# Hybrid encoder trunk on one core: parameter loads on another queue, two-operand work in another instruction, and other engine orders

## The reference

```python
h = rms(x, norm_g)
p = h @ w_in[layer]                       # 1024 x 11808, cut into the parts below
a = deltanet(conv5(p_qkv), gates(p_ab)) * silu(z_a)     # 4 heads, chunks of 64, both directions
b = neighbourhood_attention(q, k, v, rpb) * silu(z_b)   # 8 heads of 64, 16 columns
c = grouped_query_attention(rope(q), rope(k), v) * silu(z_c)
d = mlstm(q, k, v, gates(p_if)) * sigmoid(o) * silu(z_d)
m = sum over n of sigmoid(h @ w_gate[n]) * (branch[n] @ w_branch[n])
x = x + m @ w_out[layer]
```

## Time and profile before

| | |
|---|---|
| median of 3 runs | 962.58 us (962.46 to 967.27) |
| profiled execution | 968.08 us |
| its span | 966.0 us |
| TensorE busy | 903.6 us (94%) |
| VectorE busy | 660.0 us (68%) |
| ScalarE busy | 496.8 us (51%) |
| GpSimd busy | 208.6 us (22%) |
| granted TensorE clock, mean | 0.988 |

### The profile page before, as it was taken

How to read it: one execution, slowest core, us unless ns; L and a number is a source line. 1 busy time by engine, 2 the same in 40 slices (tenths; PEclk the granted TensorE clock), 3 DMA queues, 4 the chain that set the end, 5 groups by cost and what they waited for, 6 DMA issues and landing times.

```text
span 966.0 us, 18557 instructions
## 1 busy us (share of the span) xinstructions
PE 903.6 (94%) x7206; PEld 745.9 (77%) x7206; DVE 660.0 (68%) x1205; ACT 496.8 (51%) x997; POOL 208.6 (22%) x220
## 2 busy tenths in 40 slices
PE   0899989999999999999999999899999999999998
PEld 0798868787778788877879887687777777887786
DVE  0579895656437888568766989655644777875874
ACT  1546753554445466535545666344543555655452
POOL 0201521135240100322120122213334010032310
PEclk9999999999999999999989999899999999999999
DMA  7473544434339535548657346343333693443764
GB/s 214 128 231 114 179 136 130 116 91 127 118 92 215 142 98 174 143 132 213 201 153 227 101 161 208 91 131 89 88 111 110 164 208 99 142 144 100 216 196 109
DMA packets 101964, 141.03 MB, mean 146 GB/s; under 512 B 31102, under 2 KB 45558, under 8 KB 101750
## 3 DMA queue, kind: packets, MB, share of 16 engines
q1 hardware_dynamic: 97995, 138.76, 49.7%
q10 hardware_dynamic: 3883, 1.10, 0.6%
HBM read 136.67 MB, written 7.27 MB: 149 GB/s over the span
## 4 chain that ended last, share of the span: by engine, by line
PE 72%; DVE 15%; ACT 3%; DMA 3%; ACTq 2%; POOL 2%; issue 2%; SPq 1%; POOLq 0%; DVEq 0%
PE pj L764 14%; PE pj L766 13%; PE pj L765 13%; DVE w_low L1563 5%; PE pair L758 4%; PE mb L764 4%; PE mb L766 3%; PE mb L765 3%; DMA ring<-in_w_in 2%; DVE big L1632 2%; PE pair L964 2%; ACTq L719 2%; PE mb L1104 1%; PE pair L959 1%; PE mb L758 1%
## 5 line engine op out<-in xcount | busy, mean ns | idle before, releaser
L1563 DVE TENSOR_TENSOR w_low<-ring,w_high 128x512 fp32r<-128x512 f32 x460 | 324.4, 747 | 85.1 <-ACT w_high L1271 84.0
L1271 ACT ACTIVATE w_high<-ring 128x512 fp32r<-128x512 f32 x460 | 277.2, 629 | 189.0 <-PE pj L766 120.9
L764 PE MATMUL pj<-w_high,h_high 128*128 128x512 f32 x584 | 238.4, 408 | 4.9 <-DVE w_low L1563 4.9
L766 PE MATMUL pj<-w_high,h_low 128*128 128x512 f32 x584 | 228.4, 391 | 0.0
L765 PE MATMUL pj<-w_low,h_high 128*128 128x512 f32 x584 | 228.2, 391 | 0.0
L764 PEld LDWEIGHTS pj<-w_high,h_high 128*128 128x128 f32 x584 | 110.0, 188 | 33.0 <-DVE w_low L1563 7.0
L766 PEld LDWEIGHTS pj<-w_high,h_low 128*128 128x128 f32 x584 | 109.8, 188 | 24.1
L765 PEld LDWEIGHTS pj<-w_low,h_high 128*128 128x128 f32 x584 | 110.3, 189 | 21.0 <-issue 0.5
L1276 ACT ACTIVATE big<-pair 128x512 f32<-128x512 f32 (+2 forms) x136 | 61.1, 481 | 78.7 <-PE pair L948 47.1
L2058 POOL TENSOR_TENSOR big<-big,tab 128x256 f32<-128x256 f32 x40 | 35.4, 894 | 127.8 <-PE pair L948 70.3
L2156 POOL TENSOR_TENSOR zbuf<-zbuf,mid 128x512 f32<-128x512 f32 x20 | 30.5, 1532 | 102.8 <-DVE mid L1977 102.8
(11 more groups left out here) (291 smaller groups left out, 1621.5 us busy)
## 6 DMA issues: line engine op xcount, KB each, us to landing
ring<-in_w_in SPq DMA_DIRECT2D x368, 256.0 KB, 3.4
ring<-in_w_branch SPq DMA_DIRECT2D x64, 256.0 KB, 3.3
ring<-in_w_out SPq DMA_DIRECT2D x32, 256.0 KB, 3.3
big<-skew SPq DMA_DIRECT2D x32, 128.0 KB, 4.9
skew<-lines SPq DMA_DIRECT2D x16, 224.0 KB
out_x<-btm SPq DMA_DIRECT2D x8, 256.0 KB, 3.9
btm<-out_x SPq DMA_DIRECT2D x8, 256.0 KB, 5.6
tab<-in_table SPq DMA_DIRECT2D x1, 1408.0 KB, 12.3
```

The source lines that it names most:

```text
L764: mm(o, r32(a), r32(b), start=start, stop=False, skip_group_check=True)
L766: return mm(o, r32(a_low), r32(b), start=False, stop=stop, skip_group_check=True)
L1271: f(r32(part(u, 0)), ring[:, u % RAW], ACT.Copy).then_inc(w_rounded, 1)
L1563: tt(r32(part(u, 1)), ring[:, u % RAW], part(u, 0), ALU.subtract).then_inc(w_split, 1)
```

## The change

Three things are changed.

1. The loads at the start. ScalarE's queue keeps only the identity and `norm_g`. The taps go to SyncE behind unit 5. The table, the narrow columns and the ten parameters go to SyncE as well, each behind one weight unit: the table behind unit 8, the columns behind unit 9, the parameters behind units 10 to 19.
2. Every `tensor_tensor` on VectorE becomes a `scalar_tensor_tensor` that first multiplies the first operand by 1.0. This includes the 464 subtractions of L1563.
3. The orders of the four engines are other ones, in both layers (both run one and the same order).

```diff
-        def load_rows(queue, layer):
+        def load_gain(queue, layer):
             queue.dma_start(g_row, norm_g[layer][None, :].to_broadcast([P, D])).then_inc(g_row_in, 16)
+        def load_taps(queue, layer):
             queue.dma_start(rawp[0:CONV * CB, :], conv_a[layer].rearrange("j (b c) -> (j b) c", c=P)).then_inc(colp_in, 16)
...
                 for unit in range(2, RAW):
                     load_unit(sp, unit)
-                sp.dma_start(tab[:, P:n_const], table[:, P:n_const]).then_inc(table_in, 16)
+                load_taps(sp, 0)
...
                 act.dma_start(tab[:, 0:P], table[:, 0:P]).then_inc(ident_in, 16)
-                load_rows(act, 0)
-                load_cols(act, 0)
+                load_gain(act, 0)
...
                         load_unit(sp, unit)
+                        first = unit - RAW - 2
+                        if layer == 0 and 0 <= first < PARAMS + 2:
+                            if first == 0:
+                                sp.dma_start(tab[:, P:n_const], table[:, P:n_const]).then_inc(table_in, 16)
+                            elif first == 1:
+                                load_cols(sp, 0)
+                            else:
+                                load_param(sp, 0, first - 2)
...
-                    if layer == 0:
-                        for n in range(PARAMS):
-                            load_param(act, 0, n)
...
-                    tt, ts, stt, reduce = nc.vector.tensor_tensor, nc.vector.tensor_scalar, nc.vector.scalar_tensor_tensor, nc.vector.tensor_reduce
+                    ts, stt, reduce = nc.vector.tensor_scalar, nc.vector.scalar_tensor_tensor, nc.vector.tensor_reduce
+
+                    def join(o, one, other, op):
+                        return stt(o, one, 1.0, other, ALU.mult, op)
...
-                            tt(r32(part(u, 1)), ring[:, u % RAW], part(u, 0), ALU.subtract).then_inc(w_split, 1)
+                            join(r32(part(u, 1)), ring[:, u % RAW], part(u, 0), ALU.subtract).then_inc(w_split, 1)
```

Of the orders, the beginning and two places of TensorE's, and ScalarE's and VectorE's beginning:

```diff
-        turn_h.0.0 turn_h.0.1 turn_h.1.0 taps turn_h.1.1 za:0:0+4@0 za:0:4+2@0 za:0:6+2@0 za:0:0+2@1 za:0:2+4@1 za:0:6+2@1 conv:0:0+4 conv:1:0+4
-        conv:2:0+4 conv:3:0+4 gatecols c:0:0+2 gatecols_turn c:0:2+2 conv:4:0+4 cols a_turn.0 a_turn.1 conv:5:0+4 scan_v.0 c:0:4+2 c:0:6+2 c:1:0+2
...
-        t1.0.1 t1.1.1 c_qkt update.0.1 update.1.1 c_score.0.0 rows.2 b:0:6+2 t1.0.2 t1.1.2 c_turn.0.0 c_score.0.1 update.0.2 b:1:0+2 update.1.2
+        turn_h.0.0 turn_h.0.1 taps za:0:0+4@0 turn_h.1.0 turn_h.1.1 za:0:4+2@0 za:0:6+2@0 za:0:0+2@1 za:0:2+4@1 za:0:6+2@1 conv:0:0+4 conv:1:0+4
+        gatecols conv:2:0+4 gatecols_turn conv:3:0+4 c:0:0+2 c:0:2+2 conv:4:0+4 cols a_turn.0 a_turn.1 conv:5:0+4 c:0:4+2 c:0:6+2 c:1:0+2 a_qkt
...
+        rows.2 b:0:4+2 t1.1.1 t1.0.2 b:0:6+2 update.1.1 update.0.2 c_qkt t1.1.2 b:1:0+2 c_score.0.0 b:1:2+2 c_turn.0.0 c_score.0.1 t1.0.3 update.1.2
...
     "ACT": ("""
-        split+1 square.0.0 square.0.1 square.1.0 split+3
+        square.0.0 split+1 square.0.1 split+1 square.1.0 split+2
     """, """
-        split+1 square.1.1 turn_h.0.0 turn_h.0.1 turn_h.1.0 turn_h.1.1 split+1 taps split+4 take:za:0@0 take:za:0@1 split+1 small split+7
+        turn_h.0.0 turn_h.0.1 square.1.1 split+4 turn_h.1.0 turn_h.1.1 split+1 take:za:0@0 small split+4 taps split+2 take:za:0@1 split+1
...
     "DVE": ("""
-        split+3 scale.0 split+1
+        split+2 scale.0 split+2
     """, """
-        scale.1 turn_h.0.0 turn_h.0.1 turn_h.1.0 turn_h.1.1 split+5 take:za:0@0 split+4 take:za:0@1 split+6 small split+5 taps conv.0 split+3 silu.0
+        turn_h.0.0 turn_h.0.1 scale.1 split+4 turn_h.1.0 turn_h.1.1 split+1 take:za:0@0 split+2 taps split+1 small split+3 take:za:0@1 split+1 conv.0
```

More of the change, by code:

```diff
@@ L148 @@
[L148 to L151, removed]
@@ L160 @@
-        split+3 d_scan.2 split+2 d_scan.3 take:gate:1,1@1 split+2 d_sum.0 split+1 d_sum.1 split+3 take:gate:3,0@0 split+2 take:gate:3,0@1 split+5
-        d_out.0 split+1 d_out.1 split+4 y_parts.3 split+2 take:gate:3,1@0 take:gate:3,1@1 split+8 merged.0 split+3 merged.1 split+5
+        turn_h.0.0 turn_h.0.1 square.1.1 split+4 turn_h.1.0 turn_h.1.1 split+1 take:za:0@0 small split+4 taps split+2 take:za:0@1 split+1
+        take:conv:0@0 split+2 silu.0 split+2 take:conv:1@0 gatecols split+5 take:conv:2@0 split+4 silu.1 take:conv:3@0 gates_exp split+6 silu.2
@@ new lines @@
+        split+1 silu.3 split+2 cols a_turn.0 a_turn.1 a_norm.0 split+2 a_norm.1 take:conv:4@0 split+4 take:conv:5@0 take:c:0@0 take:c:0@1 split+4
+        a_qkt silu.4 silu.5 a_kkqk split+1 a_turn.2 split+3 rows.0 take:c:1@0 rows.1 take:c:1@1 c_prep split+2 solve0.0 split+6 t1.0.1 take:zc:0@0
+        split+1 take:zc:0@1 split+3 solve0.1 split+2 t1.1.1 split+2 take:b:0@0 t1.0.2 take:b:0@1 c_qkt split+3 c_score.0.0 t1.1.2 c_turn.0.0
+        c_score.0.1 split+1 t1.0.3 split+4 take:b:1@0 take:b:1@1 rows.2 t1.1.3 t1.0.4 split+2 c_score.1.0 split+1 c_turn.0.1 t1.1.4 t1.0.5 split+4
@@ L167 @@
     "DVE": ("""
-        split+3 scale.0 split+1
+        split+2 scale.0 split+2
     """, """
-        scale.1 turn_h.0.0 turn_h.0.1 turn_h.1.0 turn_h.1.1 split+5 take:za:0@0 split+4 take:za:0@1 split+6 small split+5 taps conv.0 split+3 silu.0
-        split+1 conv.1 conv.2 split+1 gates_in split+4 gates_out conv.3 silu.1 silu.2 silu.3 split+2 conv.4 split+5 a_norm.0 a_norm.1 split+6 a_scale
-        conv.5 silu.4 silu.5 split+2 gain_a split+4 rows_arg.0 rows_arg.1 split+1 rows.0 rows.1 split+3 c_prep split+3 take:zc:0@0 split+1
@@ L185 @@
-        take:branch:3,0@0 split+1 take:branch:3,0@1 split+4 merged.0 split+1 take:branch:3,1@0 merge_sum.0 take:branch:3,1@1 merge_sum.1 split+3
-        merged.1 split+3 take:out:0@0 d_scan.3 take:out:0@1 split+2
+        turn_h.0.0 turn_h.0.1 scale.1 split+4 turn_h.1.0 turn_h.1.1 split+1 take:za:0@0 split+2 taps split+1 small split+3 take:za:0@1 split+1 conv.0
+        split+3 silu.0 conv.1 split+6 conv.2 gates_in split+1 silu.1 split+4 gates_out split+2 conv.3 split+1 silu.2 silu.3 split+5 a_norm.0 split+2
@@ new lines @@
+        a_norm.1 conv.4 split+2 a_scale split+2 conv.5 silu.4 silu.5 split+6 rows_arg.0 rows_arg.1 split+1 rows.0 split+1 rows.1 split+3 c_prep
+        split+5 take:zc:0@0 split+1 take:zc:0@1 split+1 update.0.1 c_rotate.0 rows_arg.2 split+2 c_rotate.1 update.1.1 split+3 update.0.2 split+2
+        c_score.0.0 c_score.0.1 split+7 update.1.2 update.0.3 c_mix.0.0 c_score.1.0 split+1 update.1.3 split+1 update.0.4 split+2 c_mix.0.1 split+3
+        rows_arg.3 update.1.4 split+1 cols c_sum.0 c_score.1.1 rows.2 update.0.5 rows.3 split+4 c_mix.1.0 c_mix.1.1 c_sum.1 split+1 update.1.5
@@ L1909, in d_rows @@
                         dve.wait_ge(*filled(("a", s)))
-                        link(tt(mS[:, s], four(b.t), over(K(f"mask{KIND_OF[s]}"), H), ALU.add))
+                        link(join(mS[:, s], four(b.t), over(K(f"mask{KIND_OF[s]}"), H), ALU.add))
                         reduce(amx[:, s], b.t.rearrange("p (h k n) -> p h k n", h=H, k=2), X, ALU.max).then_inc(b.free, 1)
```

173 lines of the change are left out of this document (87 added, 86 removed).

## The result

The kernel after takes 925.82 us (median of 4 runs, 922.02 to 931.55) against 963.35 us of the kernel before on the same chip (4 runs, 962.46 to 967.27). The profiled execution took 924.6 us, its span is 922.5 us, 43.5 us shorter than that of before. Its mean granted clock is 1.0 (before 0.988). The other three runs of the kernel after had 0.996 (the one of 931.55 us), 0.998 and 1.0, so even this kernel doesn't keep the full clock in every execution.

The account below looks back on a forecast made before the run. The prediction took an almost full TensorE (busy 94% of the span) with a few holes as the bound. Its terms, -12.5 + 3 + 0 - 4 = -13.5 us, gave 949 us, range 937 to 960.

Parts of the forecast that it names:

- Start: Kernel start without ScalarE's DMA issues: first transpose at 14.2 us, first product about 17; -12.5 us, bounds -10 and -15.
- 2.2 us given back by the transposes of tile 1: At the start: two groups of tile 1's transposes now stand behind the first four units, giving back 2.2 us.
- Moved loads: Loads put between weights on SyncE: gatecols waits for the last parameter near 45 us; +3 us, bounds 0 and +6.
- The instruction: scalar_tensor_tensor on VectorE, mainly the subtraction L1563, costs the same as tensor_tensor; 0 us.
- rule of half throughput: Rival on VectorE: the new instruction runs at half rate, adding 245 us of VectorE, time about 1010 us; chance 0.02.
- The escape: Rival on VectorE: GpSimd doesn't hold up the new instruction; -4 us more on the path, 945, down to 938; chance 0.15.
- The orders: New step orders fill TensorE's holes behind the start, or open others; -4 us, bounds -15 and +10.
- What can be filled is at most 34.8 - 4 = 31 us: TensorE's idle time from 32 us on, less the last stores, as the most that new orders can fill.
- c_qkt's wait: TensorE's largest named wait, for L1835's rotated queries: 6.9 us for both layers, most of it filled by the new order.
- The orders do more than I can place: Rival: the new orders gain more than the forecast's term, time 930 to 941 us; chance 0.06.
- Late loads: Rival: moved loads eat the start's gain, ScalarE's splits for conv:0 up to 9 us late; 958 to 961; chance 0.10.
- a VectorE that holds TensorE in the new orders: Rival: VectorE steps placed ahead of splits hold the units behind; 18 us of new holes decide, 967 and more; chance 0.04.

Follow-up runs that it names:

- params_early: The kernel after with two parameters behind each of units 10 to 14 instead of one behind each of 10 to 19; 923.64 us, 0.9536 of before.
- best: The kernel after with tensor_tensor back and two parameters behind each of units 10 to 14; 924.63 us, 0.9571 of before.
- cqkt_late: The kernel before with c_qkt (and c_score.0.0) moved later in TensorE's order only, behind first solve updates and two more units; 975.12 us, 1.0069 of before.
- conv_early: The kernel before with the new orders only up to VectorE's conv.5, ScalarE's a_norm.1 and TensorE's conv:5; 956.08 us, 0.9887 of before.
- orders_only: The kernel before with the new orders alone, loads and instruction as before; 933.58 us, 0.9656 of before.
- mid_new: The kernel before with old orders up to mixer a's kkqk step and the new ones from rows.0 on; 953.25 us, 0.9866 of before.
- the two arrangements of c_qkt: The kernel before with c_qkt later on TensorE only (1.0069 of before), or on TensorE and ScalarE with VectorE's rotations spread (973.25 us, 1.0075).
- work_back: The kernel before with the new orders alone, but VectorE's gain_a, cols and window put back to their old places; 935.62 us, 0.9678 of before.
- front_new: The kernel before with the new orders up to mixer a's kkqk step and the old ones from rows.0 on; 953.92 us, 0.9864 of before.

## Why the prediction was wrong in size

**Start, forecast -12.5, measured -16.0 at the first product and -15.3 at the first convolution product.** The mechanism is as forecast: ScalarE's sequencer was held by DMA issues, and its computing now begins with x. The first activation came at 8.29 us, in the forecast 9.6. The table load of 1.28 us was counted behind the arrival of x, but it ran at 1.60 us, ahead of the wait. The first transpose came at 12.29 us instead of 14.2 (the other 0.6 us are a shorter way from the first activation, 4.0 us), the first product at 15.72 instead of 17. Of the 2.2 us given back by the transposes of tile 1, 15.98 - 15.33 = 0.65 us are seen. The term was 3 us too small. That an issue took 9.31 us because the loads in front of it had not moved on is not shown. With the narrow columns on SyncE's queue, the weight behind them took 2.62 us to issue and the others 0.43, so a long issue again stands behind the columns; what holds it no trace tells.

**Moved loads, forecast +3, measured +2.1.** gatecols waited 2.1 us for the last parameter, as forecast. The table landed in 6.3 us instead of 12.3, and small's splits kept ahead of TensorE. With the wait taken away (params_early, best) no gain is seen for certain.

**The instruction, forecast 0, measured 0.** The median is 684 ns at 512 floats, so the Trainium skill's rule of half throughput (Vector Engine (DVE) Microarchitecture Reference, Points that are easy to get wrong) doesn't hold in this trace. The escape didn't come either: VectorE's split has a mean of 758 ns with either instruction. This agrees with the Trainium skill (SBUF — State Buffer, Who interferes with whom), by which the contention with GpSimd depends on two SBUF inputs and not on the opcode. Both rivals are out.

**The orders, forecast -4 with bounds of -15 and +10, measured -33.** This is the step that failed: "What can be filled is at most 34.8 - 4 = 31 us", with half of it as the bound and c_qkt's wait as the value. Two things were wrong in it. First, the holes don't cost only their idle time. Behind five of them TensorE ran at half clock, by the mean clock up to 11.6 us in all, and this lies inside the 899 us called busy. The mean clock of 0.988 stood in the table and wasn't multiplied out. Second, the value was read from named waits, and the largest one, moved by itself, came back larger (cqkt_late). What the runs show in its place: the new orders up to the last convolution block close the hole between 64 and 84 us. They start VectorE's convolution work 12.5 us earlier, and fill most of the 6.8 us in which VectorE was idle between 44 and 64 us (conv_early, where the other two engines' orders change too). The orders behind that close the next holes. The accounts of orders_only close so: its span is 966.0 - 932.3 = 33.7 us shorter, of which TensorE's idle time gives 18.3 and its busy time 15.4 (up to 11.6 the clock, 3.8 not placed). Its first 32 us in the kernel before and in orders_only (TensorE's busy time is the second figure behind the window):

```profile
0.00:32.00 32.00, 4.34 (x18) 3.53 (x19) 7.21 (x12) 8.23 (x17) 5.75 (x14) 1.00 0.70 194
```

```profile
0.00:32.00 32.00, 6.05 (x20) 4.83 (x21) 7.46 (x13) 9.20 (x19) 3.88 (x12) 1.00 0.73 194
```

That is 1.7 us of idle time less at the start. So behind the start the idle time shrank by 16.5 us, somewhat more than the -15 that was taken for the bound and four times the 4 that were taken for the value, and the clock's share came on top.

**The rivals.** "The orders do more than I can place", 930 to 941, had the right sign and place and was given 0.06; even it ended 4 us above the result. Late loads and a VectorE that holds TensorE in the new orders did not come about.

What stays open is which steps of the order from rows.0 on make mid_new's 12.8 us. Only the two arrangements of c_qkt were tried alone, and both lost 7 us. mid_new changes all four engines' orders, and an earlier c_prep on GpSimd, on the path to c_qkt before, is a rival to VectorE that no run separates.

## What to carry to other kernels

Where TensorE is the bound and has holes, take windows of the engine behind it: find the stretch where that engine is full, and the idle time ahead of it is what a new order may use. A named wait is only the step at which a lag is met first, and moving that step alone can lose; follow it back along the chain, through VectorE to GpSimd here, before you choose what to move. Add to TensorE's idle time what the clock costs, at most (1 - mean granted clock) x span, since here the clock rose to full when the holes were closed.

## What the runs showed of the hardware

- The granted clock fell to half, 1.2 GHz, five times in the kernel before, for 3.4 or 6.8 us each, each time behind a stretch with idle TensorE. The traces of orders_only, work_back and the kernel after, without these holes, show no fall before the last microseconds. front_new and mid_new lose the falls at 86 and 144 us where they close the holes. A hole of about 2 us is followed by a fall in some executions and not in others (params_early and the kernel after).
- ScalarE loads its activation table while its first activation still waits for data: 1.60 us for the load, 8.29 us for the activation.
- scalar_tensor_tensor and tensor_tensor take the same time for two float32 operands of 512 elements in SBUF (684 and 687 ns), and are delayed alike by GpSimd (983 and 982 ns in the mean beside a tensor_tensor of GpSimd, 684 without). Where the new order brings such an operation beside GpSimd's sums, it shows: L1777's mean over eight is 934 ns, and the same group had 692 ns before. Six of the eight take 691 to 693 ns. The other two stand beside a sum of GpSimd of 1.67 us and take 1.66 us.
